# A mixer and 32 experts on one core: the first matrix by column halves, half its bias spread by GpSimd, and waits moved in front of the experts

## What is computed

```python
logits = xt @ w_router + b_router
top_val, top_idx = lax.top_k(logits, TOP_K)
gates = jax.nn.softmax(top_val, axis=-1)
...
hu = xblk @ w_up_gate[e] + b_up_gate[e]        # 1024 -> 2048
g, u = hu[:, :D_FF_EXPERT], hu[:, D_FF_EXPERT:]
g = jnp.minimum(g, SWIGLU_LIMIT)
u = jnp.clip(u, -SWIGLU_LIMIT, SWIGLU_LIMIT)
act = g * jax.nn.sigmoid(SWIGLU_ALPHA * g) * (u + 1.0)
return act @ w_down[e] + b_down[e]             # 1024 -> 1024
```

## Time and profile before

| | us |
|---|---|
| median of 3 runs (1777.87 to 1783.04) | 1778.39 |
| the profiled execution | 1776.7 |
| its span | 1775.0 |
| front and mixer (0 to about 520 of the span) | 520 |
| output projection, router, tables (to about 602) | 82 |
| experts (to about 1748) | 1146 |
| last sums, norm and output (to the end) | 27 |

### The profile page before, as it was taken

The page is one execution under the profiler, slowest core; times in us unless marked ns, Lnnn a source line. Parts: engine busy times, 40 slices in busy tenths (PEclk is TensorE's granted clock), DMA queues, the critical chain, the costliest instruction groups (busy, mean ns, idle before and its releaser), DMA issues.

```text
span 1775.0 us, 26529 instructions
## 1 busy us (share of the span) xinstructions
PE 1742.4 (98%) x8973; PEld 1286.6 (72%) x8973; DVE 1421.8 (80%) x1450; ACT 1140.8 (64%) x1122; POOL 315.6 (18%) x241
## 2 busy tenths in 40 slices
PE   8999999999999989999999999999999999999997
PEld 7778777777877767777777777777777777777765
DVE  4666576567665889888988898889888988898898
ACT  4544564455454567777777777777777777777783
POOL 1102201210220111112111211121112111211153
PEclk9999999999999999999999999999999999999999
DMA  7432233133126489999999999999999999999995
GB/s 209 143 96 61 82 106 106 36 106 106 36 104 249 172 260 398 391 368 383 355 371 380 367 366 365 380 367 360 374 377 366 369 369 377 369 359 374 379 337 234
DMA packets 159058, 488.44 MB, mean 275 GB/s; under 512 B 13186, under 2 KB 83122, under 8 KB 125520
## 3 DMA queue, kind: packets, MB, share of 16 engines
q1 hardware_dynamic: 151696, 471.39, 72.5%
q0 software_dynamic: 7088, 16.52, 2.7%
q10 hardware_dynamic: 240, 0.09, 0.0%
HBM read 479.43 MB, written 24.39 MB: 284 GB/s over the span
## 4 chain that ended last, share of the span: by engine, by line
PE 94%; DVE 3%; DMA 1%; ACT 1%; issue 1%; ACTq 0%; DVEq 0%
PE psum L327 28%; PE psum L329 27%; PE psum L328 27%; PE psum L988 1%; PE psum L701 1%; PE psum L731 1%; PE psum L1024 1%; PE psum L972 1%; PE psum L717 1%; DVE wL L1729 1%; PE psum L667 1%; PE psum L684 1%; DMA x2d<-xr 1%; PE psum L765 0%; PE psum L898 0%
## 5 line engine op out<-in xcount | busy, mean ns | idle before, releaser
L1729 DVE TENSOR_TENSOR wL<-wraw,wH 128x2048 fp32r<-128x2048 f32 x388 | 882.8, 2289 | 124.4 <-ACT wH L425 121.6
L425 ACT ACTIVATE wH<-wraw 128x2048 fp32r<-128x2048 f32 x388 | 743.7, 1918 | 297.5 <-PE psum L329 294.8
L327 PE MATMUL psum<-wH,xTH 128*96 128x512 f32 x1040 | 417.9, 402 | 3.6 <-DVE wL L1729 3.5
L329 PE MATMUL psum<-wH,xTL 128*96 128x512 f32 x1040 | 409.4, 394 | 0.0
L328 PE MATMUL psum<-wL,xTH 128*96 128x512 f32 x1040 | 408.8, 393 | 0.0
L327 PEld LDWEIGHTS psum<-wH,xTH 128*96 128x96 f32 x1040 | 168.3, 162 | 75.4 <-DVE wL L1729 4.5
L329 PEld LDWEIGHTS psum<-wH,xTL 128*96 128x96 f32 x1040 | 168.3, 162 | 73.0
L328 PEld LDWEIGHTS psum<-wL,xTH 128*96 128x96 f32 x1040 | 168.7, 162 | 69.7
L327 PE MATMUL psum<-wH,aTH 128*96 128x512 f32 x496 | 196.9, 397 | 0.0
L329 PE MATMUL psum<-wH,aTL 128*96 128x512 f32 x496 | 194.8, 393 | 0.0
L328 PE MATMUL psum<-wL,aTH 128*96 128x512 f32 x496 | 194.3, 392 | 0.0
(11 more groups left out here) (272 smaller groups left out, 2170.3 us busy)
## 6 DMA issues: line engine op xcount, KB each, us to landing
wraw<-in_w_up_gate SPq DMA_DIRECT2D x256, 1024.0 KB, 6.8
wraw<-in_w_down SPq DMA_DIRECT2D x128, 1024.0 KB, 7.4
fraw<-in_w_in SPq DMA_DIRECT2D x68, 512.0 KB, 4.1
yd<-in_consts SPq DMA_DIRECT2D x8, 1024.0 KB, 7.9
wraw<-yd SPq DMA_DIRECT2D x3, 2048.0 KB, 11.0
wraw<-in_w_out SPq DMA_DIRECT2D x4, 1024.0 KB, 4.9
xt<-in_x SPq DMA_DIRECT2D x4, 512.0 KB, 5.6
hres<-in_x SPq DMA_DIRECT2D x4, 512.0 KB, 5.2
```

Of the source, the lines that this page charges most:

```text
L327: nc.tensor.matmul(ps, lh, rh, start=start, stop=False)
L329: return nc.tensor.matmul(ps, ll, rh, start=False, stop=stop)
L425: nc.scalar.activation(wH[:, b % SPLIT, :], raw(b), ACT.Copy).then_inc(p_hi, 1)
L1729: V.tensor_tensor(wL[:, b % SPLIT, :], raw(b), wH[:, b % SPLIT, :].bitcast(F32), ALU.subtract).then_inc(p_lo, 1)
```

## The change

1. **Start.** The transposes of the tokens no longer wait for `vecs`; `rows` is turned after the second tile. The warm-up matmuls between the tiles are gone (9 in one go at the start, in place of 17). On DVE the tokens' scaling stands before the work on `vecs`.
2. **In front of the experts.** `row_squares` writes to a place in `cst` and has no wait; the wait for the DMA moves to DVE's `scaled_rows`, and there `route(0)` stands before `scaled_rows(2)`. The DMAs out of `xr` are issued by ACT and not by SP. The broadcast of the final gain (0.5 MB) is loaded after block 1's weights. The bfloat16 bias has only the gate half.
3. **Gates and list.** `gates_and_overflow` is cut in two. `gate_rows` stands on DVE after block 2's body and `overflow_list` after block 3's; SP's DMAs that need them come after the weights of block 4.
4. **Column halves.** A piece of `w_up_gate` is now 256 rows by 1024 columns, of the gate half (pieces 0 to 3) or of the linear half (4 to 7). PE does all of the gate half, then all of the linear half, which has no bias matmul. `silu` stands on ACT behind the split of piece 7.
5. **Linear bias.** SP loads the expert's 1024 values as two 2 KB rows into `brow`. GpSimd spreads each over 96 partitions with `partition_broadcast` into `bias_u` (a place in `cst`), once `clip_up` of the block before has read the old one. DVE's `clip_up` becomes two instructions: PSUM + 1 + `bias_u`, then the clip in place.
6. **Late blocks** on GpSimd stand between the rows of blocks 5 to 7, `dg` after them; the loops are unrolled up to there, and PE at the end waits as before.

```diff
-            warm_up(3)
-            pe.wait_ge(vec_in, 64)
-            nc.tensor.transpose(bank[0][:, 0:R_END], rows[:, :], cst[0:R_END, K_ID:K_ID + R_END]).then_inc(vecT_done, 1)
-            warm_up(5)
-            pe.wait_ge(vec_ready, 1)
+            warm_up(9)
             for j in range(NT):
...
-                warm_up((7, 1, 1, 0)[j])
+                if j == 1:
+                    pe.wait_ge(vec_in, 64)
+                    nc.tensor.transpose(vec_turned, rows[:, :], cst[0:R_END, K_ID:K_ID + R_END]).then_inc(vecT_done, 1)
...
             def row_squares(j):
                 act.wait_ge(h_ready, 2 * j + 2)
-                if j >= 2:
-                    act.wait_ge(x2_out[j % 2], 16)
-                A(xr[:, j % 2, :], hres[:, j, :], ACT.Square, accum_out=stat[:, 16 + j:17 + j]).then_inc(sd1, 1)
+                A(squares, hres[:, j, :], ACT.Square, accum_out=stat[:, 16 + j:17 + j]).then_inc(sd1, 1)
...
             def scaled_rows(j):
...
+                if j >= 2:
+                    dve.wait_ge(x2_out[j % 2], 16)
...
             def up_src(e, p):
-                return w_up_gate[0][bass.ds(e, 1), p * P:(p + 1) * P, :].rearrange("o p n -> (o p) n")
+                rows_of, cols = slice(p % 4 * 2 * P, (p % 4 + 1) * 2 * P), slice(p // 4 * FF, (p // 4 + 1) * FF)
+                return w_up_gate[0][bass.ds(e, 1), rows_of, cols].rearrange("o (k p) n -> p (o k) n", p=P)
...
+            def load_bias_row(i, e):
+                if not first(i):
+                    sp.wait_ge(b_step, BIAS_STEPS + 2 * i)
+                for n in range(2):
+                    cols = slice(FF + n * FF // 2, FF + (n + 1) * FF // 2)
+                    sp.dma_start(brow[32 * n:32 * n + 1, :], b_up_gate[0][bass.ds(e, 1), cols]).then_inc(b_in, 16)
...
                 for p in range(8):
+                    half = p // 4
+                    if p % 4 == 0:
+                        if half == 0:
+                            for n in range(2):
+                                nc.tensor.matmul(bank[n][0:BLK, :], sel[:, 0:BLK], bias[:, n * 512:(n + 1) * 512], start=True, stop=False)
+                            if not first(i):
+                                pe.wait_ge(xTl_ready, 2 * i + KD)
+                        elif not first(i):
+                            pe.wait_ge(ucl_ready, 2 * i - 1)
                     wait_split(pe, k, b0 + p)
                     slot = (b0 + p) % SPLIT
+                    for kk in range(2):
+                        kb = 2 * (p % 4) + kk
...
+                        for n in range(2):
+                            last = mm3(bank[2 * half + n][0:BLK, :], xTH[:, kb, :], xTL[:, kb, :], wH[:, slot, half_piece(kk, n)],
+                                       wL[:, slot, half_piece(kk, n)], half == 1 and kb == 0, kb == KD - 1)
...
                     high(act, i, b)
+                    if b == 7:
+                        silu(i)
...
-                V.tensor_scalar(ucl[0:BLK, :], hu[0:BLK, FF:2 * FF], 1.0 + LIMIT, 1.0 - LIMIT, ALU.min, ALU.max).then_inc(ucl_ready, 1)
+                dve.wait_ge(b_step, BIAS_STEPS + 2 * i + 2)
+                V.scalar_tensor_tensor(out=ucl[0:BLK, :], in0=hu[0:BLK, FF:2 * FF], scalar=1.0, in1=bias_u[0:BLK, :], op0=ALU.add,
+                                       op1=ALU.add).then_inc(ucl_ready, 1)
+                dve.wait_ge(ucl_ready, 2 * i + 1)
+                V.tensor_scalar(ucl[0:BLK, :], ucl[0:BLK, :], 1.0 + LIMIT, 1.0 - LIMIT, ALU.min, ALU.max).then_inc(ucl_ready, 1)
...
+            def spread_bias(i):
...
+                gp.wait_ge(b_in, rows_in)
+                if not first(i):
+                    gp.wait_ge(ucl_ready, added)
+                    gp.wait_ge(xg_in, gathered)
+                if not isinstance(i, int) or i > 2:
+                    gp.wait_ge(y_out, scattered)
+                for n in range(2):
+                    G.partition_broadcast(bias_u[0:BLK, n * (FF // 2):(n + 1) * (FF // 2)], brow[32 * n:32 * n + 1, :],
+                                          BLK).then_inc(b_step, 1)
+                    gp.wait_ge(tri_wr_ready, 2)
+                    gp.wait_ge(b_step, (half, whole)[n])
```

More of the change, by code:

```diff
@@ L46 @@
 BODY = 12
-BIAS_STEPS = 6
+BIAS_STEPS = 5
 BLK = 96
@@ L557, in _ @@
             load_piece(1, 0, up_src(1, 0))
-            rows_out(3)
             load_body(1, 1)
+            sp.wait_ge(wr_in, 48)
+            sp.dma_start(fgain[:, :], final_norm_gain.rearrange("(a n) -> a n", a=1).to_broadcast([P, D])).then_inc(wr_in, 16)
+            for e in range(2, SETTLED + 1):
+                load_body(e)
             sp.wait_ge(over_ready, 1)
@@ L986, in up_part @@
                     pe.wait_ge(pos_free, 1)
[L987 to L990, removed]
                 for p in range(8):
-                    if first(i):
-                        pe.wait_ge(xTl_ready, p + 1)
+                    half = p // 4
[7 more added lines that the diff above has]
+                            pe.wait_ge(ucl_ready, 2 * i - 1)
                     wait_split(pe, k, b0 + p)
                     slot = (b0 + p) % SPLIT
-                    for n in range(4):
-                        cols = slice(n * 512, (n + 1) * 512)
-                        last = mm3(bank[n][0:BLK, :], xTH[:, p, :], xTL[:, p, :], wH[:, slot, cols], wL[:, slot, cols], False, p == 7)
+                    for kk in range(2):
+                        kb = 2 * (p % 4) + kk
+                        if first(i) and half == 0:
+                            pe.wait_ge(xTl_ready, kb + 1)
+                        for n in range(2):
+                            last = mm3(bank[2 * half + n][0:BLK, :], xTH[:, kb, :], xTL[:, kb, :], wH[:, slot, half_piece(kk, n)],
+                                       wL[:, slot, half_piece(kk, n)], half == 1 and kb == 0, kb == KD - 1)
                     last.then_inc(p_used, 1)
@@ L1412, in _ @@
             high(act, 0, 10)
+            table_ahead(ACT.Silu, 1)
             high(act, 0, 11)
+            silu(0)
             high(act, 1, 0)
-            table_ahead(ACT.Silu, 1)
             x_high(1, used(up_at(0), 8))
-            silu(0)
             high(act, 1, 1)
@@ L1962, in _ @@
             clip_up(0)
+            select(1)
             x_low(1)
-            select(1)
             swiglu(0)
@@ L2169, in scatter, with rows_of @@
                                       bounds_check=last_assignment, oob_is_err=False).then_inc(y_out, 16)
-            for i in range(1, 4):
-                gather(i, NBC * i)
+            gather(1, NBC)
+            spread_bias(1)
+            gather(2, NBC * 2)
+            spread_bias(2)
+            gather(3, NBC * 3)
             gp.wait_ge(zeros_out, 16 * NH)
             scatter(0, 0)
-            with gp.Fori(2, NE - 2) as i:
+            def rows_of(i):
+                spread_bias(i + 1)
                 gather(i + 2, NBC * (i + 2))
                 scatter(i - 1, NBC * (i - 1))
-            scatter(LATE[0] - 1, NBC * (LATE[0] - 1))
             def late_block(i, code):
@@ L2214, in _ @@
                                 ALU.mult).then_inc(place_set, 1)
+            gp.wait_ge(place_set, 8 + TOPK)
+            with gp.Fori(SETTLED + 4, NE - 2) as i:
+                rows_of(i)
+            spread_bias(NE - 1)
+            scatter(LATE[0] - 1, NBC * (LATE[0] - 1))
             gp.wait_ge(y_out, 16 * LATE[0])
```

113 lines of the change are left out of this document (77 added, 36 removed).

## The result

The changed kernel takes 1789.22 us (median of 8 runs, 1780.09 to 1792.44) against 1778.61 before: ratio 1.0046, 95% interval 1.003 to 1.0061. It is slower, where 1756.3 was forecast. The profiled execution has a span of 1790.3 us against 1775.0, so 15.3 us are to be found.

A forecast was written before the change was run, and what follows sets the result against it. PE was taken as the bound, 94% of the chain of waits. The terms 12.9 + 5.3 + 6.4 - 0.7 + 0 - 1.8 = 22.1 us, from the median 1778.39, gave 1756.3 us; range 1751 to 1765.

The forecast's parts named there:

- The steady blocks: Expert blocks 2 to 31: two bias matmuls fewer, period 35.0 us for 35.44, 12.9 us won.
- GpSimd's room: GpSimd waits 18.5 us a block before the gather's copy; spreads and late blocks were taken to fit there at no cost.
- The price of a spread: Linear bias on GpSimd: 0.6 us a spread, 1.2 a block, 1.35 at the far end; no cost to DVE.
- the cover of 1.9: First piece of a block: of 3.0 us between DVE's split and PE's use, 1.9 stay after the change.
- The third rival: Before the experts: the DMA out of `xr` again takes 12.81 us, route(1) 8 us late, 1764 us; chance 0.1.
- the route: Before the experts: PE's wait of 3.59 us for DVE's route goes, with half the half-clock time; 5.3 us won.
- Gates and list: Near 643 us: PE's wait of 3.48 us behind DVE's gates and list goes, with half-clock time; 6.4 us won.
- block 1's start: PE already waits for DVE there; the clip in place adds 0.68 us, a loss of 0.7.
- The start: Start of the kernel: first projection at 14.8 for 17.05, between 2.2 us won and 1.2 lost; taken as zero.
- the rule of a low default: Start of the kernel: only activity lifts the clock, so fewer warm-ups would cost the larger price, 3.4 us.
- The last block: `silu` among splits and DVE's extra 0.68 us before the multiplication: loss between 0.7 and 3.5 us, taken as 1.8.
- DMA: Rival in the expert blocks: transfers become the bound at 35.4 us a block, steady gain lost, 1769 us; chance 0.09.

The follow-up runs named there:

- experiments 1 and 3: The changed kernel with GpSimd's late blocks and diagonal behind the loop again: 1762.81 us; or with their TENSOR_SCALARs on VectorE, in blocks 27 to 30: 1761.10 us.
- small_again: Repeat of the changed kernel with late TENSOR_SCALARs on VectorE, gather before spreads, SP's small transfers two blocks later: 1756.24 us, ratio 0.9871.
- list_back: The kernel of `small_again` with VectorE's gates and list back in block 0, in one piece as before the change: 1761.56 us, ratio 0.9897.

## Why the prediction was wrong

- **The steady blocks** were right: 35.01 us for 35.0, in every kernel, even with four spreads a block.
- **The step that failed is GpSimd's room.** "It waits 18.5 us a block before the copy that leads the gather, and both spreads could take that long before rows came late", and, as another move at no cost, "the late blocks on GpSimd, with reloads of its code, use its 18 us of idle time a block". The same room was spent twice, and both spenders were mis-sized. The spreads were put at 0.6 us each and took 14.5 the pair. Nor could they use the idle time, as they may not start before VectorE has read the old bias; all that they take came off the gather's lead, and of 21 to 24 us some 5 remained. Onto these (more, once VectorE pauses and lets spreads run in 0.8 us each) came three pieces of late work, 30, 25 and 35 us long, over half of it changes of code, which the prediction named ("reloads of its code") and gave no price. The second was still hidden, the first and the third were not. The kernel before had all this behind the last gather. Its cost was 27.7 us, of which experiments 1 and 3 give back 26 to 28.
- **The price of a spread was looked for on the wrong side.** The prediction took the 2.32 us of the earlier trace rows as VectorE held by GpSimd and asked only what VectorE loses. It loses some 0.8 us a block (from 960 to 1315 the split has 2321 ns for 2289, and `actv` 1.67 us for 1.21), within the cover of 1.9; its idle time is 2.2 us a block, not 3.0. GpSimd loses 13. The Trainium skill ("SBUF — State Buffer", Who interferes with whom) says that it is issue order that decides who blocks. I read from it that an engine whose two-input instructions follow one another without a pause wins nearly always, and the trace agrees as far as that: 11.17 us for a spread that takes 0.80 when VectorE is idle. It does not show that GpSimd waits for a pause: that spread ends at 1018.40, inside a run of six splits from 1008.86 to 1022.72. How VectorE and GpSimd take turns inside such a run stays open.
- **The third rival** (a wait in front of the experts) didn't come: the route gave 4.7 us for 5.3 (5.4 in `small_again`), with a wait of 0.43 us in place of 3.59.
- **Gates and list** are worth what was said (6.4 less 0.7 for block 1's start; `list_back` gives 6.5 in that block), but the change gets 2.4, and other kernels with the spreads first get between 4.6 and nothing. A new wait of some 4 us for gathered rows, at 648, took the place of the old one: the second gather now stood behind block 1's spreads, and its copy of the indices, beside VectorE's splits, took 17.3 us. With the gather first block 1 drops to some 36.2 us, 6.1 below before.
- **The start**: 2.3 us won, the good end of the term, where I took zero. The clock was full at the first projection of the change, so the rule of a low default, which the prediction has from the Trainium skill ("TensorE: Matmul & The Clock Gate", What's actually happening), cost nothing there; in two of eleven other traces of this start the clock was at 0.50 near it.
- **The last block**: 2.1 lost from its start to the end, with 0.4 of gain in it, so 2.5 for 1.8. PE's wait before the transposes is 3.0 us, as forecast, and the stretch at half clock behind it, which the far end of the term held, came: 0.50 for 3.4 us from 1746.2.
- **DMA** went from a share of 0.98 to 1.00, pieces of `w_up_gate` land in 9.1 us for 6.8, and the steady period doesn't feel it; the small transfers cost 5.3 us in blocks 5 and 6, which no term had.
- With the late work, the gather and SP's small transfers moved, the kernel measures 1755.5 and 1756.2 us. That this meets the 1756.3 of the forecast is in part luck. In the trace of `small_again` (20.4 us below before, for the 22.1 of the sum) the start gives 2.1 us more than the sum has and block 1 0.4 more, while the small transfers take 3.3, in no term, and the last block 1.1 more. The other terms came out within 0.2 us; the one taken as free decided the sign.

## What to carry to other kernels

An engine's idle time is one budget: write down every piece that a change puts on it, in its order, and ask of each what stands in front of the next transfer that somebody waits for. In this kernel a wide instruction on GpSimd cost what VectorE left it, 0.80 to 15.58 us, and not its own length, so put what others need (a gather) in front of it, and what uses another kind of instruction, with its change of code, behind the last such transfer or on another engine. A wait that guards 4 KB on a queue guards everything queued behind it: here eight weight pieces.

## What the runs showed of the hardware

- GpSimd beside VectorE's back to back splits: the same spread of one row to 96 x 512 took 0.80, 2.50, 3.37, 8.97, 11.17 or 15.58 us, among others, and a copy of 128 x 2 took 0.18 and, in block 1, 17.30 us (17.31 in three more traces). The long copy of the change's trace, and VectorE's splits beside its end (it ends at 642.50, two splits of some 2.25 us after 637.97; VectorE had no pause from 621.50 on):

```profile
625.20 17.30 POOL L2210 COPY ixg<-tab 128x2 int32<-128x2 int32 x1
```

```profile
637.97 6.72 DVE L1757 TENSOR_TENSOR wL<-wraw,wH 128x2048 fp32r<-128x2048 f32 x3
```

- A change between spread and TENSOR_SCALAR on GpSimd took 7.2 to 10.3 us without any work in the trace of the change, and 6.5 to 10.3 over all five traces that have such changes. The Trainium skill ("GPSIMD Engine Reference", Instruction dispatch) gives approximately 6 us for the first call of a freshly loaded kernel; here every one of the 21 took longer, in the change's trace with the DMA engines at a share of 0.70 to 1.03 beside it. Each begins with MODIFY_POOL_CONFIG.
- After the small transfers (among them one of 2048 gates and one of 128 numbers) the DMA engines moved 124 GB/s for 9 us at a share of 1.09, where 372 is the mean of ten steady blocks. No run takes these transfers apart.
- The granted clock fell to 0.50 for 3.4 us in block 0 in five of thirteen traces of changed kernels, with the same instructions and waits of PE in front of it, and cost 1.6 us.
